# The end of a feed-forward: two down projections kept back in place of three, and tile 0's transposes behind tile 1's last projection

## The reference

```python
def _swiglu(x, w_in, w_out):
    gate, up = jnp.split(x @ w_in, 2, axis=-1)
    return (jax.nn.silu(gate) * up) @ w_out

x = _layernorm(DEEPNORM_ALPHA * x + FFN_RESIDUAL * _swiglu(x, ffn_w_in[i, 0], ffn_w_out[i, 0]),
               ln_g[i, 0], ln_b[i, 0])
...   # mixers; then the second feed-forward, in the same form
e = jax.nn.sigmoid(x @ ple_gate_w[i] + ple_gate_b[i]) * (p[i] @ ple_w[i])
x = _layernorm(DEEPNORM_ALPHA * x + e, ln_g[i, 3], ln_b[i, 3])
```

## Time and profile before

| | us |
|---|---|
| median of 3 runs | 1436.04 |
| lowest and highest run | 1435.56, 1437.43 |
| the profiled execution | 1432.55 |
| its span | 1430.7 |
| PE busy in it | 1409.7 |

### The profile page before, as it was taken

One profiled execution on the slowest core, in us unless ns is written; L12 is line 12 of the kernel. 1 busy time (PEld: TensorE's weight loads), 2 busy tenths in 40 slices (PEclk: granted clock), 3 DMA queues, 4 the chain that ended last, 5 costly groups with the idle time before them and its releaser, 6 DMA issues.

```text
span 1430.7 us, 20859 instructions
## 1 busy us (share of the span) xinstructions
PE 1409.7 (99%) x8906; PEld 1260.8 (88%) x8906; DVE 1067.0 (75%) x1165; ACT 667.5 (47%) x653; POOL 53.7 (4%) x100
## 2 busy tenths in 40 slices
PE   8999999999999999999999999999999999999997
PEld 7888879999999888888878888899999998888885
DVE  4766686889887876666977666868997868666687
ACT  5444435663545444344444444447545464443441
POOL 0400000000000020000100000000000001000001
PEclk9999999999999999999999999999999999999999
DMA  7685545546554576564565555554456365655541
GB/s 266 222 256 187 177 149 176 177 132 218 161 169 148 192 230 224 186 202 156 173 234 179 200 195 193 177 174 151 155 199 175 97 228 181 225 176 199 203 158 59
DMA packets 168044, 263.18 MB, mean 184 GB/s; under 512 B 8958, under 2 KB 101456, under 8 KB 167952
## 3 DMA queue, kind: packets, MB, share of 16 engines
q1 hardware_dynamic: 163616, 249.66, 52.4%
q0 software_dynamic: 4336, 12.20, 2.8%
HBM read 260.77 MB, written 1.05 MB: 183 GB/s over the span
## 4 chain that ended last, share of the span: by engine, by line
PE 92%; DVE 5%; ACT 1%; DMA 0%; SPq 0%; issue 0%; DVEq 0%; ACTq 0%
PE ps L1373 20%; PE ps L1277 18%; PE ps L1279 18%; PE ps L1278 18%; PE ps L1375 10%; PE ps L1485 3%; DVE big L929 2%; PE ps L1303 1%; PE ps L1308 1%; PE ps L1305 1%; DVE wlo L782 1%; PE ps L1344 1%; ACT whi L549 1%; DMA raw<-in_ffn_w_in 0%; DVE big L865 0%
## 5 line engine op out<-in xcount | busy, mean ns | idle before, releaser
L782 DVE TENSOR_TENSOR wlo<-raw,whi 128x2048 fp32r<-128x2048 f32 x230 | 521.9, 2289 | 219.0 <-ACT whi L549 218.8
L549 ACT CAST whi<-raw 128x2048 fp32r<-128x2048 f32 x230 | 438.0, 1911 | 373.7 <-PE ps L1279 242.6
L1373 PE MATMUL ps<-xhl,whi 128*128 128x512 f32 x1280 | 446.9, 392 | 2.6 <-DVE S L797 2.4
L1375 PE MATMUL ps<-xhl,wlo 128*128 128x256 f32 x1280 | 357.9, 280 | 0.0
L1277 PE MATMUL ps<-xhl,whi 128*128 128x256 f32 x1056 | 298.2, 282 | 0.0
L1278 PE MATMUL ps<-xhl,whi 128*128 128x256 f32 x1056 | 296.1, 280 | 0.0
L1279 PE MATMUL ps<-xhl,wlo 128*128 128x256 f32 x1056 | 296.1, 280 | 0.0
L1373 PEld LDWEIGHTS ps<-xhl,whi 128*128 128x128 f32 x1280 | 240.3, 188 | 56.8 <-DVE S L797 2.7
L1375 PEld LDWEIGHTS ps<-xhl,wlo 128*128 128x128 f32 x1280 | 240.5, 188 | 1.4
L1277 PEld LDWEIGHTS ps<-xhl,whi 128*128 128x128 f32 x1056 | 199.0, 188 | 1.3 <-issue 1.0
L1278 PEld LDWEIGHTS ps<-xhl,whi 128*128 128x128 f32 x1056 | 199.0, 188 | 0.1
(11 more groups left out here) (249 smaller groups left out, 1493.8 us busy)
## 6 DMA issues: line engine op xcount, KB each, us to landing
raw<-in_ffn_w_in SPq DMA_DIRECT2D x172, 512.0 KB, 5.0
raw<-in_w_in SPq DMA_DIRECT2D x140, 512.0 KB, 4.5
raw<-in_ffn_w_out SPq DMA_DIRECT2D x88, 512.0 KB, 4.2
raw<-in_w_br SPq DMA_DIRECT2D x32, 512.0 KB, 5.0
raw<-in_w_out SPq DMA_DIRECT2D x16, 512.0 KB, 4.4
raw<-in_ple_gate_w SPq DMA_DIRECT2D x16, 512.0 KB, 4.7
gv<-in_ln_g POOLq DMA_DIRECT2D x8, 512.0 KB, 4.4
b_bc<-in_ln_b POOLq DMA_DIRECT2D x8, 512.0 KB, 6.1
```

Source lines behind the costliest of these rows:

```text
L549: nc.scalar.copy(whi[:, slot, :], raw[:, source, :]).then_inc(whi_made, 1)
L782: nc.vector.tensor_tensor(wlo[:, slot, :], raw[:, source, :], whi[:, slot, :].bitcast(F32), ALU.subtract).then_inc(wlo_made, 1)
L1373: nc.tensor.matmul(ps[:, 2 * q + u, :], w[:, k, u, P * q:P * q + P], xhl[:, :, 4 * kk + k, :], start=kk == 0 and k == 0, stop=False, skip_ ...
L1375: ins = nc.tensor.matmul(ps[:, 2 * q + u, 256:512], v[:, k, u, P * q:P * q + P], xh[:, 4 * kk + k, :], start=False, stop=kk == 1 and k == ...
```

## The change

`gu_at` and `wo_at` are renumbered, so that down chunk 8 is number 28 and gate_up(10) has 29 and 30; 31 and 32 stay. On PE both tiles of down(8) go between gate_up(9) and gate_up(10), with the loop's pattern. Behind gate_up(10) stand down(9, 0), down(10, 0), down(9, 1), down(10, 1), and then `turn_x` of tile 0. `late()` stands behind down(9, 0). SP loads in the order of the new numbers. The lists of ACT and DVE are not changed in the text, but their targets follow `gu_at`. All of it applies to each of the four feed-forwards.

```diff
 def gu_at(j):
 
-    return 0 if j == 0 else 28 if j == NFF - 1 else 3 * j - 1
+    return 0 if j == 0 else 3 * j - 1
 
 
 def wo_at(j):
 
-    return 3 * j + 4 if j < NFF - 3 else 22 + j
+    return 3 * j + 4 if j < NFF - 2 else 22 + j
...
-                    if 1 <= j < NFF - 2:
+                    if 1 <= j < NFF - 1:
                         chunk(c0 + wo_at(j - 1), wout[:, 2 * j - 2:2 * j, :], (2, 1024))
-                for j in range(NFF - 3, NFF):
+                for j in range(NFF - 2, NFF):
                     chunk(c0 + wo_at(j), wout[:, 2 * j:2 * j + 2, :], (2, 1024))
...
-                for j in range(2, NFF - 2):
+                for j in range(2, NFF - 1):
                     gate_up(j)
                     for t in range(TT):
                         down(j - 1, t)
-                gate_up(NFF - 2)
                 gate_up(NFF - 1)
-                for j in range(NFF - 3, NFF):
+                for j in range(NFF - 2, NFF):
                     down(j, 0)
-                    if j == NFF - 3 and late is not None:
+                    if j == NFF - 2 and late is not None:
                         pe.wait_ge(h_made, 2 * (n0 + NFF))
                         late()
-                for j in range(NFF - 3, NFF - 1):
+                for j in range(NFF - 2, NFF):
                     down(j, 1)
                 if late is not None:
                     pe.wait_ge(pc_made, DEPTH)
                 turn_x(version + 1, 0, xtok)
-                down(NFF - 1, 1)
```

## The result

The changed kernel takes 1450.83 us (median of 5 runs, 1450.46 to 1452.37) against 1436.04 us before (5 runs): a ratio of 1.0105 (95% interval 1.0094 to 1.0117), 14.8 us slower. The forecast was 1452.1 us, in a range of 1446 to 1457.

What follows compares the result with a forecast made beforehand. PE, busy 1409.7 of 1430.7 us, was taken to bound the kernel, new waits paid in full. Losses at four feed-forward ends, 3.6 + 4.2 + 4.1 + 4.2 = 16.1 us, on 1436.04 gave 1452.1 us, range 1446 to 1457.

Steps and rivals of the forecast that it cites:

- The bound and the ends' tightness: Whole kernel: PE is busy 1409.7 of 1430.7 us; waits at feed-forward ends covered, five of at most 0.3 us.
- E + 14.0: Old kernel: PE reaches tile 0's transposes 14.0 us after the first down projection behind the last gate/up block; no slack.
- Hidden block: Before projection 10 of tile 0: PE waits 1.9 us, one down projection now covering; 0.3 us in layer 0's first feed-forward.
- E': Changed kernel's time mark: start of the first down projection behind the last gate/up block, at each feed-forward's end.
- Tile 0's transposes: After the last down projections: start 13.4 us behind the last gate/up block, 0.3 us waiting, hiding most of 1.9 us.
- Tile 1's chain: Tile 1's residual queues behind tile 0's low halves; waits of 0.95 us before its transposes, 1.7 us before embedding(1).
- Rival 1: Tile 1's side is covered: its residual doesn't wait behind tile 0's low halves, only 9.9 us lost, 1446; chance 0.06.
- The lists of waits and of busy time: Profile after: new PE waits on lines L833, L870, L593, L879, 0.3 to 1.9 us; PE busy 1409 to 1411 us.
- The sum: Losses at the four ends, 3.6 + 4.2 + 4.1 + 4.2 = 16.1 us, added to 1436.04: 1452.1 us.
- E comes 5.6 us later: 24 matmuls of down projection 8 go ahead of the last gate/up block, delaying the mark behind it by 5.6 us.
- Rival 3: Clock falls to 1.2 GHz behind each end: a 5.7 us block takes twice that, 4 x 5.7, 1475; chance 0.02.
- Rivals 2 and 4: 2: further conversion ahead of each end's chain, 2.29 us each, 1461, 0.05; 4: tile 1's chain starts sooner, 1434.8, 0.05.

Runs made afterwards that it cites:

- e4: Changed kernel with the four kept-back projections ordered by block (9 of both tiles, then 10 of both): 1451.52 us, ratio 1.0112.
- e2: Kernel before, three projections kept back, with only tile 0's transposes moved behind tile 1's last projection: 1442.92 us, ratio 1.0049.
- e8: Changed kernel with tile 1's first residual and statistics put ahead of tile 0's low halves on DVE: 1447.78 us, ratio 1.0088.
- e1: Changed kernel with tile 0's transposes in their old place, ahead of tile 1's last projection: 1459.86 us, ratio 1.0169.
- e5: Changed kernel with kept-back projections ordered by block and DVE's conversion of chunk 34 behind tile 0's xtok: 1461.75 us, ratio 1.0185.
- e7: e1 with 10 unused products of constants ahead of the transposes, keeping PE busy in most of the wait: 1455.88 us, ratio 1.0148.
- e3: Changed kernel with DVE's conversion of chunk 34 back behind tile 0's xtok: 1450.67 us, ratio 1.0106.

## Why the prediction was right

**The bound and the ends' tightness: right.** PE had no slack to give, and of each chain the wait that ended last was paid in full. E + 14.0 for the transposes against xtok at the same moment was the reading on which the forecast rested.

**Hidden block: right, and rightly not added up.** The wait is 1.7 us three times and 0.2 once (forecast 1.9 and 0.3, counted to the matmul's start, E' + 4.66 against 4.7). By e4 it costs nothing by itself, as the prediction's step on tile 0's transposes said.

**Tile 0's transposes: right.** They start at E' + 13.39 in the second feed-forwards and, in the first ones, at 204.56 - 189.91 = 14.65 (14.56 forecast) and 916.67 - 903.14 = 13.53 (13.4), where a small conversion (L996) that I left out stands ahead of the residual. Fresh tokens follow 1.4 us later, as at the layers' boundary.

**Tile 1's chain: right.** The waits are 0.7 to 0.8 us at its transposes (0.95 forecast) and 1.5 us at embedding(1) (1.7). e2 and e8 show it by adding it alone and by shortening it. Rival 1, which had this part covered, would have given 9.9 us.

**The lists of waits and of busy time: partly wrong.** On L870 ahead of tile 0's transposes the forecast had 0.3 to 0.9 us at all ends; the page has 1.3 us in layer 0's first feed-forward, 0.2 in layer 1's first, and none in the second ones. The two new waits of 0.5 us on L593 didn't come: one of 0.17 us did, and the row as a whole fell from 1.6 to 1.1 us. PE's busy time was to stay at 1409 to 1411 us and is 1417.3, half for the longer records beside waits and half for the clock, as shown above.

**The sum: 1.3 us too high.** The term that was mis-sized is "E comes 5.6 us later". It came 5.3 us later, since the seam between two gate/up blocks went. The earlier trace rows had it in plain sight (22.5 us for two blocks), and I used the number without asking why it wasn't 22.2. With 4 x 0.3 off, the forecast of the ends is 14.9, and 14.8 was measured.

**Rival 3, the clock: not at this kernel's ends, but the reason for leaving it out was weak.** The clock term was put at 0 from the 1.00 of one execution behind its longest wait. In the changed kernel's profile that very stretch is followed by a clock of 0.50, and e1 and e5 show low stretches at three of four ends. That the changed kernel's own ends kept their clock is known for the profiled execution alone; the mean clock of its five runs (0.994 to 0.996) lies in the range of the kernel before (0.994 to 0.998). So this part of the forecast came out with some luck. The price in the rival, 5.7 us an end, was too high as well: e1's low stretch in layer 0's second feed-forward makes that end 1.5 us longer than layer 1's, which has the same waits. The Trainium skill ("TensorE: Matmul & The Clock Gate", "HAM oscillation") says that idle gaps between bursts can bring the slower clock back; e1 and e7 agree. No run here separates the part of the transposes from that of the waits.

**Rivals 2 and 4.** No further conversion got ahead of a chain: the DVE order was the one that the code writes. Tile 0's low halves were done at about 16 and not before E' + 11.7.

## What to carry to other kernels

When work is moved out of the tail of a stage, list what each piece was covering, on every engine's queue, and count from a common mark; waits in one chain don't add up, and removing the one that the profile shows (e4: 5.3 us) may give nothing. Then look who is late next: an engine that works in order passes a delay of one tile on to the other. A wait's price can also be more than its length, because the clock can fall behind it. Here it did so behind waits of 1.3 to 4.1 us, and behind others of the same length it didn't; a profile with a clock of 1.00 throughout doesn't exclude it for the next execution.

## What the runs showed of the hardware

The clock fell behind waits of quite different length: 4.1, 3.0 and 2.9 us (e1), 2.8 and 1.9 (e5), 2.2 (e4), and in e3 behind the 1.3 us at the layers' boundary, where the kernel before kept it (a matmul at the low clock has 0.63 us here, instead of 0.39):

```profile
734.07 1.32 PE L1344 MATMUL ps<-kc,xtok 128*128 128x128 f32 x8 [1.33 <-DVE xtok L870]
...
736.18 0.63 PE L1303 MATMUL ps<-whi,xhl 128*128 128x512 f32 x1
```

A low clock also came without any wait: in the changed kernel's profile it falls at 1009.4 us, in the mixers of layer 1, where PE was busy all the time, just behind 8 matmuls on operands that weren't split (L1483, 1.97 us) and a few small transposes. The kernel before ran the same instructions at 994.6 us with the clock at 1.00. Of the eleven profiles it is the only one without a fall at this place, in one layer or in both.

The two falls in the changed kernel's profile cost 1.5 and 1.65 us; the one in e4's third end cost 0.4, since tile 1's transposes no longer had to wait behind it. There are none to six of them in a profiled execution, and that fits the spread of the runs: for the kernel before 1432.06 us at a mean clock of 0.998 and 1437.63 us at 0.994. (Runs without a profile show only their mean clock.) A comparison of two single executions was off by 3.5 us, nearly all for this reason, a quarter of the effect; marks within the traces, between which no low stretch lies, agree to 0.1 us.
